# One more tile's gates scattered by GpSimd, and a reworked schedule around it, in a hybrid decoder layer

## The reference

```
h = x @ w_in                       # one projection for everything below
q, k, v = ...                      # 12 heads x 64, rotary positions on q and k
y_a = dilated attention            # three (window, dilation) patterns, combined by log-sum-exp
qkv = silu(causal_depthwise_conv(qkv_b, dn_conv))
y_b = gated DeltaNet(qkv)          # 6 heads x 128, chunks of 64
merged = sigmoid(g0) * (y_a @ w_branch_attn) + sigmoid(g1) * (y_b @ w_branch_delta)
x = layer_norm(ALPHA * x + merged @ w_out)
# PEER: 8 heads, the 16 best of 128 x 128 single-neuron experts for every token
q = x @ w_query;  s = q . sub_keys;  experts, gate = top16 of top16 x top16 sums, softmax
act = gelu(x . expert_down[experts])
x = layer_norm(ALPHA * x + sum(gate * act * expert_up[experts]))
```

## Time and profile before

| | us |
|---|---|
| median of three runs | 4230.79 (4228.75 to 4232.65) |
| profiled execution, its own time | 4235.46 |
| its span | 4233.6 |
| PE busy in it | 3690.2 (87%) |
| DVE busy in it | 2963.3 (70%) |
| POOL busy in it | 2119.9 (50%) |
| ACT busy in it | 1350.2 (32%) |
| mean DMA rate | 229 GB/s |
| mean granted TensorE clock | 0.937 |

### The profile page before, as it was taken

The page is one execution under the profiler, slowest core; times in us unless marked ns, Lnnn a source line. Parts: engine busy times, 40 slices in busy tenths (PEclk is TensorE's granted clock), DMA queues, the critical chain, the costliest instruction groups (busy, mean ns, idle before and its releaser), DMA issues. The chain is left out here.

```text
span 4233.6 us, 61324 instructions
## 1 busy us (share of the span) xinstructions
PE 3690.2 (87%) x22032; PEld 3429.6 (81%) x22032; DVE 2963.3 (70%) x5578; ACT 1350.2 (32%) x2384; POOL 2119.9 (50%) x1447
## 2 busy tenths in 40 slices
PE   8786778998987989898979898989887999899997
PEld 8785777998887878888979898989786777777776
DVE  2432545488754477676798877866555898889899
ACT  3443322222224533211213656565112222222221
POOL 0013420023365445334358776788884666666664
PEclk8997889999998999999989999999998999999999
DMA  4354324467885545767768786899987888888885
GB/s 149 122 168 124 98 100 140 154 227 243 300 277 160 131 146 164 264 234 268 275 184 248 214 270 210 248 296 277 317 257 257 303 313 298 289 304 317 299 313 210
DMA packets 457721, 970.58 MB, mean 229 GB/s; under 512 B 75008, under 2 KB 223792, under 8 KB 456496
## 3 DMA queue, kind: packets, MB, share of 16 engines
q1 hardware_dynamic: 310064, 565.25, 40.2%
q0 software_dynamic: 147456, 402.85, 30.3%
HBM read 802.50 MB, written 137.52 MB: 222 GB/s over the span
## 5 line engine op out<-in xcount | busy, mean ns | idle before, releaser
L2033 POOL DMA_INDIRECT ring<-in_down_rows,ids x384 | 500.2, 1303 | 717.0 <-DVE coef L2049 464.4
L2385 PE MATMUL r_psd<-x1h,r_dh 128*128 128x320 f32 x2048 | 658.6, 322 | 77.0 <-DVE r_dl L2317 77.0
L2385 PE MATMUL r_psd<-x1l,r_dh 128*128 128x320 f32 x2048 | 646.1, 315 | 0.0
L2385 PE MATMUL r_psd<-x1h,r_dl 128*128 128x320 f32 x2048 | 645.2, 315 | 0.0
L2049 DVE CUSTOM_DVE_ANT_0 ring<-ring,ring_x 128x1024 f32<-128x1024 f32 x384 | 472.4, 1260 | 191.2 <-DMA ring<-in_down_rows,ids 184.3
L2647 PE MATMUL e_psy<-e_uh,e_Ch 128*128 128x512 f32 x1280 | 512.4, 400 | 93.7 <-DVE e_Cl L2568 93.6
L452 PE MATMUL p_ps<-p_xh,p_wh 128*128 128x320 f32 (+1 forms) x1392 | 459.8, 330 | 104.9 <-DVE p_wl L367 104.7
L2289 POOL DMA_INDIRECT W<-r_put,r_place x256 | 466.8, 1823 | 88.6 <-issue 76.6
L2647 PE MATMUL e_psy<-e_ul,e_Ch 128*128 128x512 f32 x1280 | 507.8, 397 | 0.0
L2647 PE MATMUL e_psy<-e_uh,e_Cl 128*128 128x512 f32 x1280 | 506.6, 396 | 0.0
L2385 PEld LDWEIGHTS r_psd<-x1h,r_dh 128*128 128x128 f32 x2048 | 397.3, 194 | 85.5 <-DVE r_dl L2317 85.5
(11 more groups left out here) (378 smaller groups left out, 8264.8 us busy)
## 6 DMA issues: line engine op xcount, KB each, us to landing
hand<-in_down SPq DMA_DIRECT2D x128, 512.0 KB
hand<-in_up SPq DMA_DIRECT2D x128, 512.0 KB
input_w<-in_w_in SPq DMA_DIRECT2D x116, 512.0 KB, 3.7
act<-r_act SPq DMA_DIRECT2D x128, 320.0 KB
e_W<-W SPq DMA_DIRECT2D x127, 320.0 KB
W<-r_W SPq DMA_DIRECT2D x24, 1024.0 KB
hand<-act SPq DMA_DIRECT2D x64, 320.0 KB
e_araw<-act SPq DMA_DIRECT2D x64, 320.0 KB
```

The source lines that it names most:

```text
L2033: self.nc.gpsimd.indirect_dma_start(out=self.ring[j % NGB][:], out_offset=None, in_=table, in_offset=bass.IndirectOffsetOnAxis(ap=self.g.i ...
L2385: ins = nc.tensor.matmul(psd[n][:, h, 0:HD], a[c % DEEP][:, k, :], b[:, k, h * HD:(h + 1) * HD], start=(k == 0 and m == 0), stop=(k == KD ...
```

## The change

Six things are changed together. (1) Tile 5 moves from PLACED to SCATTERED: 384 scatters instead of 256, from chunk 7 to chunk 121 and evenly, and two groups of one-hot work (chunks 59 to 74 and 83 to 98) instead of three (31 to 46, 55 to 70, 79 to 94). Tile 2 is routed at chunk 42 instead of 48. (2) 256 instead of 222 rows are used in the late part, and 256 instead of 290 in R, two in every chunk; before it was about 1.8 in each of the first 76 chunks and then 3. (3) The projection has three weight buffers, its loops are written out, and SP issues the load of a block before the store of the block before. (4) In the early part all six pairs are rotated on POOL and stacked by SP during projection blocks 16 to 51, into six sets of stacks, and the early attention does neither. In the late part the stacks come at blocks 42 and 44, the routing of tiles 0 and 1 takes blocks 0 to 5 and 6 to 19, and the rows begin at block 7. (5) E has three buffers for `up`, `act` and W, and a ring of nine gathered rows instead of ten. (6) Coefficients and GELU of tiles 0 and 1, and the loads of the gathered tiles' tokens, are issued sooner.

```diff
-SCATTERED = (3, 4)
-PLACED = (5, 6, 7)
+SCATTERED = (3, 4, 5)
+PLACED = (6, 7)
...
+            def load(b):
+                sp.wait_ge(w_lo, START + b - RAW + 1)
+                sp.dma_start(wraw[b % RAW][:], g.w_in[b]).then_inc(ld_w[b % RAW], 16)
+
+            def store(b):
+                sp.wait_ge(out_ready, START + b + 1)
+                sp.dma_start(g.hT[b, :, part.cols], out[b % 2][:]).then_inc(stored[b % 2], 16)
+
...
+            def stack(pair, h):
+                tiles = g.stacks[pair] if early else g.stack0
+                for n, parts in enumerate(((0, 1), (2, 2), (3, 3))):
+                    for half, which in enumerate(parts):
+                        sp.dma_start(tiles[h][n][half * AD:(half + 1) * AD, :].bitcast(F32),
+                                     g.rope_out[which][h * AD:(h + 1) * AD, :].bitcast(F32)).then_inc(g.next["stacked0"], 16)
...
+            GAP = 6
+            for b in range(N_IN):
+                if b + RAW < N_IN:
+                    load(b + RAW)
+                if b >= 1:
+                    store(b - 1)
...
+                    pair, step = (b - N_ATT + 2) // GAP, (b - N_ATT + 2) % GAP
+                    if 0 <= pair < AT and step == 0:
+                        if pair == 0:
+                            stored_to(2 * AT)
+                        sp.wait_ge(sem("split"), START + 2 * pair)
+                        for n in range(4):
+                            load_rope(pair, n)
+                    if 0 <= pair < AT and step == GAP - 1:
+                        sp.wait_ge(sem("split"), START + 2 * pair + 2)
+                        for h in range(2):
+                            stack(pair, h)
+                else:
+                    if 6 <= m < 10:
...
+            if early:
+                pool.wait_ge(sem("table"), START + 32)
+                for pair in range(AT):
+                    pool.wait_ge(sem("ld_q"), START + 160 * pair + 160)
+                    for n in range(4):
+                        multiply(pair, n)
+                    pool.wait_ge(g.next["stacked0"], START + 192 * pair)
+                    for n in range(2):
+                        add_and_split(pair, n)
+                return
+            ROPE = 36
...
-            ROPE = 44
+            ROPE = 36
...
-                pe.wait_ge(stacked[par], START + 48 * HPT * (i - par) + 96 * HPT)
+                if early:
+                    pe.wait_ge(stacked[0], START + 96 * HPT * i + 96 * HPT)
+                else:
+                    pe.wait_ge(stacked[par], START + 48 * HPT * (i - par) + 96 * HPT)
...
-PROJECT_ROWS, CHUNK_ROWS, MERGE_ROWS, NORM_ROWS, SCORE_ROWS = 108, 4, 4, 2, 4
+PROJECT_ROWS, CHUNK_ROWS, MERGE_ROWS, NORM_ROWS = P, 6, 5, 3
 BEFORE_MERGE = PROJECT_ROWS + CHUNK_ROWS * ND
 BEFORE_NORM = BEFORE_MERGE + MERGE_ROWS * (KD - 1)
 BEFORE_SCORES = BEFORE_NORM + NORM_ROWS * ND
-EARLY_ROWS = BEFORE_SCORES + SCORE_ROWS * (2 * PH - 2)
+EARLY_ROWS = 2 * P
...
-    for x, c in enumerate(placed_pieces(0, 9)):
+    for x, c in enumerate(placed_pieces(0, 6)):
         pieces[c].append((0, x))
-    for x, c in enumerate(placed_pieces(9, 12)):
+    for x, c in enumerate(placed_pieces(6, 14)):
         pieces[c].append((1, x))
-    first, last = 10, N_IN - 2
+    first, last = 7, N_IN - 2
     uses = [range(0)] * N_IN
     for n in range(last - first):
...
-    ROUTED = (3, 4, 5, 6, 2, 7)
-    ROUTE, ROUTE_FROM = 14, (0, 7, 14, 28, 48, 62)
+    ROUTED = (3, 4, 5, 2, 6, 7)
+    ROUTE, ROUTE_FROM = 14, (0, 7, 14, 28, 42, 62)
...
-    split_at = (routed_in[SCATTERED[0]] + PK - 6) // 2
-    scatters = spread(evenly(routed_in[SCATTERED[0]] + 1, split_at, P) + evenly(0, PK - 6 - split_at, P))
+    begin = routed_in[SCATTERED[0]] + 1
+    scatters = spread(evenly(begin, PK - 6, NS * P))
+    assert all(scatters[routed_in[t]].stop <= n * P for n, t in enumerate(SCATTERED))
     scatters += [range(NS * P, NS * P)] * (PK - len(scatters))
     routing = ROUTE_FROM[-1] + ROUTE
     late_rows = len(ROW_ORDER) - EARLY_ROWS
-    sooner = late_rows * 47 // 100
-    uses = spread(evenly(0, routing, sooner) + evenly(0, PK - 1 - routing, late_rows - sooner) + [0])
+    uses = spread(evenly(0, PK - 1, late_rows) + [0])
...
-    NGU = 10
+    NGU, RAW = 9, 3
...
-        uraw = g.hand[0:2]
-        araw = [g.hand[2][:, 0:TD], sb("e_araw1", [P, TD])[:]]
-        Wt = [sb(f"e_W{u}", [P, TD]) for u in range(2)]
+        uraw = g.hand
+        araw = [gathered.x[:, 0:TD]] + [sb(f"e_araw{u}", [P, TD])[:] for u in (1, 2)]
+        Wt = [sb(f"e_W{u}", [P, TD]) for u in range(RAW)]
...
             for c in range(2, NCH):
-                sp.wait_ge(sem("C_lo"), START + c - 1)
-                load(c, c % 2)
+                if c >= RAW:
+                    sp.wait_ge(sem("C_lo"), START + c - RAW + 1)
+                    load(c, c % RAW)
```

446 lines of the change are left out of this document (224 added, 222 removed).

## The result

The changed kernel takes 4316.6 us (median of 4 runs, 4302.9 to 4326.2) beside 4229.8 for the kernel before: ratio 1.0202, 95% interval 1.0174 to 1.0231. The interval leaves no doubt that it is slower, by about 2%. Forecast were 4260 and a range of 4165 to 4325. The sign and the stage that decides were right, the size was not: +87 us instead of +29. The time lies inside the wide range, and outside the 4235 to 4290 that the forecast gave itself. Its profiled execution took 4317.7 us, its span is 4315.9, 82.3 more than before.

The account below looks back on a forecast made before the run. POOL's stream was taken to set R's pace, DVE to bound E. The terms -18 - 45 - 15 + 20 + 97 - 10 = +29 on the median 4230.8 gave 4260 us, range 4165 to 4325.

Parts of the forecast that it names:

- R: Stage R: POOL's stream of 384 scatters and about 228 gathers sets the pace; +97 us, bounds -40 and +146.
- E: Last stage: third buffer gives back part of DVE's 41.7 us wait, one gather slot fewer costs something; -10, bounds -30 and +8.
- the late DeltaNet stage: Late DeltaNet: five chunks with two more rows each at 1.1 us a row; +11 us.
- the gap before the merge: Blanking of W for one more tile: transfers without anyone late for them; nothing.
- the merge and the norm: Late merge with 7 more rows and norm with 5, each as long at most; +9 us together.
- lower bound of -40: Stage R if POOL did not bind at all and only PE's side counts: -40 us.
- The early and late projection and the early attention: Early projection -18 us, late projection -15, early attention -45 with nothing left to wait for in the stacks.
- SP bursts: Early projection: SP's twelve stack transfers in one burst delay a block six times; 14 us, +13 in the sum.
- A: Rival, faster: POOL no longer bounds R, or DVE keeps up; R at +3, sum -65, 4166 us; chance 0.28.
- point of decision: Rival A decides from R below +60, where the sum falls under -8.5.
- B: Rival, no change: R at +97, gains at their lower ends (-50, -50, -30), sum -23; window 4222 to 4239; chance 0.10.
- C: Rival, slower: early projection +21 instead of -18, 4299 us; chance 0.12 together with the tail's prices in R.

Follow-up runs that it names:

- the first part alone: The kernel before, with only tile 5 moved to the scattered tiles (even scatters, tile 2 routed earlier): 4390.3 us, ratio 1.0382.

## Why the prediction failed, step by step

The forecast added up to +29 us, and 82 came in the profile, 53 more. Four steps hold 48 of them: the late DeltaNet stage (14 too little), the gap before the merge (8), the merge and the norm (6) and E (20). R was 10 too low, and the rest nearly cancels. The term that decides, R, had the right mechanism and nearly the right size.

**R, +97, measured +107.** The reading of the tail held: POOL's stream sets R, the scatters stretched 113 us (forecast 104). A scatter cost 2.12 us where 2.03 was taken, nearer to the tail's 2.17, and a gather 1.47 where 1.55 was taken, so part of the one error took back the other. The chunk of 9.9 us "throughout" is there: 1141.8/115 = 9.9. What the forecast does not show is what is in this sum. The runs part the +107 into -71 (everything else that changes in R, with tile 5 placed) and +178 (the exchange). The forecast priced the two as one, and its lower bound of -40, for a POOL that does not bind, left the second out: with tile 5's scatters gone and no one-hots in their place R is 93 us shorter than before.

**Late DeltaNet, +11, measured +25.** This step failed: "1.1 us a row", from the earlier trace rows, is the mean of four rows, and it was carried over to the fifth and sixth. These cost 2.5 us each: a chunk takes (1671.1 - 1485.1)/4 = 46.5 us, not 43.7. With the two gathers behind the selections on POOL a row costs (232.5 - 226)/10, about 0.6 us. The forecast looked at DVE alone, and the row's gather on POOL was not priced.

**The gap before the merge, 0, measured +8.3.** "Transfers without anyone late for them; nothing" failed. Someone was: the stage's last store stands behind the last two blankings. That 50% more of it does this is shown by the first part alone (9.5 to 16.5), by placing tile 5 (17.8 to 11.2) and by moving it (17.8 to 8.2).

**Merge and norm, +9, measured +15.** The stages grew 4.2 and 2.3; the gap between them 8.5, which goes with five rows a merge block (15.2 to 18.8 us in all runs with them, 8.5 to 9.8 with four). It was not in the sum. That the gathers in flight are what the norm stage waits for is read from one timeline.

**E, -10, measured +10.** This step failed with its sign: the third buffer was to give back part of the 41.7 us in which DVE waits for high parts. They fell only to 34.1, and the buffer gives nothing (990.7 us with nine slots and two). "One gather slot fewer costs something" was in the text and its size was not worked out: about 9 us over all the kernels, 7 in the pair that differs in it and the buffer.

**The early and late projection and the early attention, -78 in all, measured -79.** No wait for a stack is left in the attention, and its granted clock is 0.78 instead of 0.63. Convolution blocks take 98.4/18 = 5.5 us where 5.2 was forecast:

```profile
86.30:119.50 33.20, 33.20 (x192) 33.04 (x191) 3.94 (x8) 1.00 0.55 186
127.80:226.20 98.40, 85.53 (x447) 81.27 (x445) 9.60 (x35) 0.95 0.66 197
```

The early projection's -18 is partly luck. The forecast's SP bursts, +13 (14 in its own line before the sum), had the right effect on the sum and the wrong cause: one block in six is late, mostly 8.5 to 10.2 us, but splitting the stacks changed nothing. The rotation explains 8.6 us of it; what else holds that block stays open.

**The rivals.** A fell: scatters hardly shortened, 1.79 us on the mean against 1.82 over the whole of R before, the emptier DMA of R (share 0.76 instead of 0.82) and fewer one-hots on DVE notwithstanding. Gathers did shorten, from 1.29 to 1.15 us on the mean, for a reason that no run shows; on 228 of them that is some 30 us and not enough for A. Its point of decision was right: with R at 1079 the kernel is faster. B needs gains of -50, -50 and -30 in three stages; they were -18, -41 and +10. C gave 4299 and so came nearer to the time than the forecast, but by a cause that is not there: it needs an early projection of +21, and that was -18. The forecast's own window, 4240 to 4285 in the chances and 4235 to 4290 behind them, was too small, and not for R but for the four terms above, 14 + 8 + 6 + 20 = 48 us. (The text on the change, ahead of the forecast, says that tile 2 is routed from chunk 42; by the list of `ROUTED` it is chunk 28, and tile 6 from 42. Nothing of the forecast rests on it.)

## What to carry to other kernels

Before moving work to an engine that looks half idle, look for the stretch in which it has nothing but issue gaps, and price the work there: 22 us on three engines were exchanged for 200 on one. For every instruction added to a stream ask what stands behind it, on each engine and queue that it has a share in; a row cost 0.6, 0.9, 1.3 or 2.5 us by its place. Undo a bundled change part by part: without one of its edits this one is 2.2% faster than the kernel before instead of 2.0% slower.

## What was not expected of the hardware

- A single-element-per-partition scatter with add costs POOL as much as a gathered row of 4 KB, or more: 1.79 us on the mean against 1.13 to 1.18, with 0.3 us of issue after each.
- Three gaps between stages go by the last transfers before them: 8.2 or 17.8 us by the zeros ahead of the last store in SP's queue, 9.3 or 17.5 by the rows of the last merge block, 7.8 or 30.7 by zeros written behind the early stage.
- DVE's taps of the convolution take 759 ns on the mean with POOL's rotation in the stage and 654 without; in all it cost the stage 8.6 us, much less than the 62 us that POOL worked on these 50 instructions.
